# A decoder layer's expert picks: every pick loaded as one u|v double row, with a Gelu and a coefficient of its own

## What is computed

```python
def peer_ffn(xn, w_q, sub_keys, u_tab, v_tab):
    ...
        top_s, top_i = lax.top_k(s, K)                  # K = 16, for both halves of a head
        cand = top_s[:, :, 0, :, None] + top_s[:, :, 1, None, :]
        best_s, best_j = lax.top_k(cand.reshape(C, Hh, K * K), K)
        ...
        expert = ia * PEER_KEYS + ib
        g = jax.nn.softmax(best_s, axis=-1)
        u = u_tab[expert]
        a = jax.nn.gelu(jnp.einsum('cd,chkd->chk', xc, u).astype(jnp.float32), approximate=False)
        coeff = (g * a).astype(xc.dtype)
        return jnp.einsum('chk,chkd->cd', coeff, v_tab[expert])
```

## Time and profile before

| | |
|---|---|
| median of three runs | 3797.99 us (3793.36 to 3814.47) |
| span of the profiled execution | 3789.9 us, 8.1 below that median; its own time outside the trace is not listed |
| busy: TensorE, VectorE, ScalarE, GpSimd | 77%, 66%, 34%, 37% of the span |
| moved | 1297.10 MB, 342 GB/s over the span |
| queue of the gathers | 1073.83 MB, 72.2% of 16 engines' span |

### The profile page before, as it was taken

How to read it: one execution, slowest core, us unless ns; L and a number is a source line. 1 busy time by engine, 2 the same in 40 slices (tenths; PEclk the granted TensorE clock), 3 DMA queues, 4 the chain that set the end, 5 groups by cost and what they waited for, 6 DMA issues and landing times.

```text
span 3789.9 us, 34958 instructions
## 1 busy us (share of the span) xinstructions
PE 2933.6 (77%) x8920; PEld 1517.5 (40%) x8920; DVE 2484.4 (66%) x5699; ACT 1298.0 (34%) x3333; POOL 1420.4 (37%) x1367
## 2 busy tenths in 40 slices
PE   8797866984886598989689797787878777766665
PEld 6655533431443355555344343333333333322222
DVE  0321218786876477767437888877887887788765
ACT  1212312221121244444234544444443454344333
POOL 0000003443776376657423333333333333333332
PEclk9897888997898799999899999999989999999999
DMA  7844156777998999999889999999999999999998
GB/s 298 274 147 184 57 215 214 238 263 283 346 338 327 352 369 341 363 352 355 333 318 369 401 411 417 409 414 415 411 407 421 413 405 407 421 410 414 417 411 351
DMA packets 274454, 1297.10 MB, mean 342 GB/s; under 512 B 27888, under 2 KB 63088, under 8 KB 180464
## 3 DMA queue, kind: packets, MB, share of 16 engines
q0 software_dynamic: 195120, 1073.83, 72.2%
q1 hardware_dynamic: 74384, 203.74, 14.4%
q10 hardware_dynamic: 4752, 17.30, 1.2%
HBM read 1231.07 MB, written 63.70 MB: 342 GB/s over the span
## 4 chain that ended last, share of the span: by engine, by line
DMA 31%; issue 7%; DVE 5%; PE 4%; ACT 3%; POOL 0%; POOLq 0%; DVEq 0%; SPq 0%; ACTq 0%
DMA s_ring<-peer_uv,s_expert 17%; DMA e_more_slots<-peer_uv,s_expert 10%; PE e_acc L503 3%; DVE e_part L427 1%; PE e_product L1859 1%; DMA e_more_slots<-peer_v,s_expert 1%; DMA next_h<-e_h 1%; DMA e_h<-norm_ffn_row 1%; DMA s_scratch<-norm_final_row 1%; DVE s_ring L394 1%; ACT L341 1%; ACT s_diagonal L324 0%; ACT s_gate L343 0%; DVE s_dots L394 0%; DVE e_more_slots L394 0%
## 5 line engine op out<-in xcount | busy, mean ns | idle before, releaser
L503 PE MATMUL e_acc<-s_ring,s_diagonal 128*128 128x512 f32 (+1 forms) x2168 | 898.8, 543 | 379.6 <-ACT s_diagonal L324 352.8
L394 DVE CUSTOM_DVE_ANT_0 s_ring<-s_ring,e_x_copy 128x1024 f32<-128x1024 f32 x548 | 666.6, 1217 | 221.9 <-DMA s_ring<-peer_uv,s_expert 215.1
L503 PEld LDWEIGHTS e_acc<-s_ring,s_diagonal 128*128 128x128 f32 x2168 | 396.5, 199 | 943.5 <-ACT s_diagonal L324 587.5
L278 POOL DMA_INDIRECT s_ring<-peer_uv,s_expert x462 | 437.5, 947 | 783.1 <-DVE e_part L427 551.8
L278 POOL DMA_INDIRECT s_ring<-peer_u,s_expert x331 | 377.4, 1140 | 449.9 <-DVE s_expert L1796 230.8
L503 PE MATMUL e_acc<-e_more_slots,s_diagonal 128*128 128x512 f32 (+1 forms) x948 | 387.4, 536 | 153.9 <-ACT s_diagonal L324 146.3
L278 POOL DMA_INDIRECT s_ring<-peer_v,s_expert x325 | 373.2, 1148 | 332.0 <-PE e_acc L503 94.9
L341 ACT ACTIVATE s_dots<-s_dots 128x1 f32<-128x1 f32 x704 | 142.2, 202 | 961.3 <-DVE s_dots L394 959.0
L324 ACT ACTIVATE s_diagonal<-s_ident,s_gate 128x128 f32<-128x128 f32 x949 | 371.2, 399 | 223.0 <-PE e_acc L503 100.1
L278 POOL DMA_INDIRECT e_more_slots<-peer_uv,s_expert x231 | 217.6, 942 | 413.8 <-DVE e_part L427 273.5
L394 DVE CUSTOM_DVE_ANT_0 s_ring<-s_ring,s_x 128x1024 f32<-128x1024 f32 x245 | 299.5, 1222 | 104.6 <-DMA s_ring<-peer_u,s_expert 69.2
(11 more groups left out here) (233 smaller groups left out, 3618.5 us busy)
## 6 DMA issues: line engine op xcount, KB each, us to landing
w_in_kept<-w_in SPq DMA_DIRECT2D x8, 1104.0 KB, 11.8
w_in_gained<-w_in_kept SPq DMA_DIRECT2D x8, 1104.0 KB, 10.2
p_w_in<-w_in_gained SPq DMA_DIRECT2D x8, 1104.0 KB, 19.0
f_w_big<-w_mem_kv SPq DMA_DIRECT2D x4, 2048.0 KB, 19.2
f_w_big<-peer_w_q_t SPq DMA_DIRECT2D x2, 4096.0 KB, 17.9
peer_scores<-f_stage_s SPq DMA_DIRECT2D x16, 512.0 KB, 8.5
e_mem_scores<-mem_scores SPq DMA_DIRECT2D x2, 4096.0 KB, 14.6
e_mem_values<-mem_values SPq DMA_DIRECT2D x2, 4096.0 KB, 25.0
```

The source lines that it names most:

```text
L278: pool.indirect_dma_start(out=to, out_offset=None, in_=table, in_offset=bass.IndirectOffsetOnAxis(ap=self.expert[c % PICK_BUFFERS][:, k:k ...
L394: dve.tensor_tensor_reduce(row, row, x[:, :], 1.0, 0.0, ALU.mult, ALU.add, self.dots[:, k:k + 1]).then_inc(self.u_used, 1)
L503: last = pe.matmul(self.acc[:, at:to], self.diagonal[:, made % DIAGONALS, :], row[:, at:to], start=(n == group[0]), stop=(n == group[-1]))
```

## The change

- All 1024 picks come as pairs: ROWS is u0, v0, u1, v1, ...; there is no lead any more, and the tables peer_u and peer_v are gone.
- The ring holds pairs. Stages have extra slots of their own: 2 in the selection, 6 in the projection, 0 in the attention, 4 in the last. There is one semaphore for each pair of slots.
- Every pick has its Gelu and its coefficient by coeff_alone; GELU_AT and COEFF_AT are gone.
- In projection and attention VectorE adds V directly behind the product of the same pick (add_to_h). In the last stage it adds one pick later, as before.
- ScalarE gets two more places in the projection, 3 and 6. One bound of the first choices goes from 45 to 46.

```diff
-LEAD = 22
-PAIRS_FROM = 331
-ALONE_FROM = PAIRS_FROM // TOPK * TOPK
-ROWS = [("u", g) for g in range(LEAD)]
-for _g in range(PAIRS_FROM - LEAD):
-    ROWS += [("u", LEAD + _g), ("v", _g)]
...
+ROWS = [(kind, g) for g in range(TOTAL_PICKS) for kind in "uv"]
...
-            table = self.io["peer_uv" if paired else "peer_u" if kind == "u" else "peer_v"]
...
+            to = self.ring[:, slot:slot + 2, :] if slot < RING else self.more_slots[:, slot - RING:slot - RING + 2, :]
+            pool.indirect_dma_start(out=to.rearrange("p s d -> p (s d)"), out_offset=None, in_=self.io["peer_uv"],
                                     in_offset=bass.IndirectOffsetOnAxis(ap=self.expert[c % PICK_BUFFERS][:, k:k + 1], axis=0)
-                                    ).then_inc(self.row_loaded[self.slot[n]], 16)
+                                    ).then_inc(self.row_loaded[slot], 16)
...
-            if n in GELU_AT:
-                i = GELU_AT[n]
-                h = i % PEER_HEADS
-                at = slice(TOPK * h, TOPK * (h + 1))
-                act.wait_ge(self.u_used, TOPK * (i + 1))
-                act.activation(self.active[:, at], self.dots[:, at], ACT.Gelu).then_inc(self.activated, 1)
...
-            if kind == "v" and self.pe_columns(n) > 0:
-                if g >= ALONE_FROM:
-                    self.coeff_alone(g)
-                elif g % TOPK == 0 or n - 2 < self.stages[self.stage_of[n]][0]:
-                    act.wait_ge(self.coeff_ready, g // TOPK + 1)
...
+            if kind == "v":
+                self.coeff_alone(g)
+                if self.pe_columns(n) > 0:
+                    made = self.pe_through[n]
+                    need(act, self.v_pe, made - DIAGONALS)
...
-            elif self.mode(n) == "split":
-                self.wait_row(dve, n)
-                dve.wait_ge(self.coeff_ready, g // TOPK + 1)
...
+                first, end, mode = self.stages[self.stage_of[n]]
+                add = self.add_to_h if mode == "split" else self.add_part
+                if mode == "split":
+                    add(n)
+                    continue
...
+    def add_to_h(self, n):
+
+        dve = self.nc.vector
+        g = ROWS[n][1]
+        rest = slice(self.pe_columns(n), D)
+        self.wait_row(dve, n)
+        dve.wait_ge(self.coeff_made, g + 1)
+        self.wait_h(g // PICKS, self.dve_through[n] - 1)
+        dve.scalar_tensor_tensor(self.h[:, rest], self.row(n)[:, rest], self.coeff(g), self.h[:, rest], ALU.mult,
+                                 ALU.add).then_inc(self.v_dve, 1)
...
                 if more:
                     square_x(t + 1)
+                if woven:
+                    beside(stream.scalar, t, 3)
+                if more:
                     keep_x_t(t + 1)
...
+                if woven:
+                    beside(stream.scalar, t, 6)
                 act.wait_ge(q_turned, t + 1)
...
-STAGES = [(PICK_FIRST, "pe", D), (PROJECT_REST, "split", 0), (ATTEND_REST, "split", BANK), (len(ROWS), "pe", 3 * D // 4)]
+STAGES = [(PICK_FIRST, "pe", D, 2), (PROJECT_REST, "split", 0, 6), (ATTEND_REST, "split", BANK, 0), (len(ROWS), "pe", 3 * D // 4, 4)]
```

More of the change, by code:

```diff
@@ L127, in __init__ @@
         self.nc, self.io = nc, io
-        self.stages = [(start, until, mode) for start, (until, mode, _) in zip([0] + [u for u, _, _ in stages], stages)]
-        self.columns = [columns for _, _, columns in stages]
-        assert all(mode == "split" or columns == D or s == len(stages) - 1 for s, (_, mode, columns) in enumerate(stages))
+        self.stages = [(start, until, mode) for start, (until, mode, _, _) in zip([0] + [stage[0] for stage in stages], stages)]
+        self.columns = [columns for _, _, columns, _ in stages]
+        self.extra = [extra for _, _, _, extra in stages]
+        assert all(mode == "split" or columns == D or s == len(stages) - 1 for s, (_, mode, columns, _) in enumerate(stages))
         self.ident = sb("s_ident", [P, P])
@@ L171, in __init__ @@
         pe = dve = 0
-        free = list(range(RING))
+        free = list(range(0, RING, 2))
         last_in = {}
-        wide_from = self.stages[-1][0] + RING
         for n in range(len(ROWS)):
             s = next(i for i, (start, until, _) in enumerate(self.stages) if start <= n < until)
+            start, until, _ = self.stages[s]
             kind = ROWS[n][0]
@@ L231, in wait_row @@
     def wait_row(self, eng, n):
-        first = n - 1 if n >= PAIRS_AT and ROWS[n][0] == "v" else n
-        eng.wait_ge(self.row_loaded[self.slot[first]], 16 * self.loads[first])
+        eng.wait_ge(self.row_loaded[self.slot[n] // 2 * 2], 16 * self.loads[n])
     def group(self, c, s):
@@ L1549, in pick_buffers, with pick_chunks @@
     return b
-def pick_chunks(nc, io, stream, chunks, events, until, last):
+def pick_chunks(nc, io, stream, chunks, events, until, stage, last):
     with ExitStack() as ctx:
         sb, ps, sem = allocators(nc, ctx, f"_{chunks[0]}")
-        if last:
-            stream.more_slots = sb("e_more_slots", [P, WIDE_RING - RING, D])
+        if stream.extra[stage]:
+            stream.more_slots = sb("e_more_slots", [P, stream.extra[stage], D])
         mem_scores = sb("e_mem_scores", [P, DT, D])
```

113 lines of the change are left out of this document (42 added, 71 removed).

## The result

The changed kernel takes 4144.24 us (4 runs, 4138.07 to 4148.4) against 3799.88 us before: a ratio of 1.088, with an interval of 1.085 to 1.092. The forecast was 4030 us, in a range from 3880 to 4120. The side was right, the size was not: 344 us were lost where 232 were forecast, and the time lies above the range.

The account below looks back on a forecast made before the run. VectorE bounds selection, row transfers the last stage; projection and attention run close to the transfers' limit. Selection -10, projection +55, attention +187, last 0 make +232; 3789.9 + 232 + 8 = 4030 us, range 3880 to 4120.

Parts of the forecast that it names:

- The ring's pieces: Attention unit as closed loop: Exp, turning, copy, table load, Gelu, table load; 5.6 to 6.9 us, 2.5 per further V row.
- its two prices: Attention: two table loads of 1.28 us per unit, and a 2.5 us turn over VectorE per further V row.
- Rival (a): Projection and attention: row supply decides, pairs make the 490 rows 57 us faster, time 3740; chance 0.07.
- Rival (b): Attention: the 170 stalls fall into VectorE's idle time, only the projection pays, about 3850; chance 0.12.
- Rival (c): Attention: a stop as long as the load follows each of 136 further table loads, 174 us more, 4200; chance 0.03.
- ScalarE now follows VectorE pick by pick and gets 19 more table loads ... they hide: Selection: the loads, 24 us, hide because ScalarE is busy only 70 of 356 us; the stage changes by -10.
- the gain of the eleven products: Selection: VectorE does 75 products instead of 86, at 1.22 us each, 13 us less on the bounding engine.
- the projection, +55: Projection: a chunk takes 66.5 us against 55.6 because additions wait for their own coefficients; five chunks, between 0 and +90.
- the attention's sum: Attention: eighty units 500, further V rows 205, ends 38 and 25, between chunks 12, restarts 16; 796 against 609, +187.
- TensorE does not stand in the way: Attention: TensorE's 6.5 us at 1024 columns are less than the 9.4 of a unit with two V rows.
- four pairs in flight are enough: Attention: one pair is wanted every 4 to 5 us and takes 2.6 us of transfer and 1.25 on GpSimd.
- the middle parts: Whole kernel: the inner portions of the terms' bounds, giving 3910 to 4120; the range's start was lowered to 3880.

Follow-up runs that it names:

- e_copy: The changed kernel with a plain copy in place of the Gelu of picks 0 to 319, so they exchange no table; ratio 1.038.
- e_lag: The changed kernel with VectorE's addition of V in projection and attention one pick later; ratio 1.051.
- e_pelag: The changed kernel with TensorE's V multiplications of picks 0 to 74 (selection) one pick later in its order; ratio 1.087.
- e_beach: The kernel before, keeping single rows and its lead of 22 products, with a Gelu and coefficient per pick and ScalarE's two new projection places; ratio 1.045.
- e_copylag: The changed kernel with a plain copy for the Gelu of picks 0 to 319 and VectorE's addition one pick later in projection and attention; ratio 1.028.
- e_turn: The changed kernel with VectorE's picks ahead of the copy to a_mixed_t in the unit of the turning; ratio 1.088.
- e_ring3: The changed kernel with three pairs of row slots in the attention in place of four; ratio 1.098.
- e_copylag3: The changed kernel with copy for Gelu (picks 0 to 319), addition one pick later, and three pairs of row slots in the attention, not four; ratio 1.068.

## Why the prediction was right and wrong

**Right: what would bound each stage, and how.** The last stage stayed (-6, forecast between -20 and +20). In the attention VectorE's addition waits for ScalarE, the DMA share falls (0.69, forecast 0.75), 168 table loads stand on ScalarE (forecast 165). The ring's pieces are as worked out: 5.74 us at 512 columns with one pick (5.6), 9.58 at 1024 with two (9.4), a further pick 2.55 (2.5). e_copy and e_lag take its two prices away one at a time. Rival (a) fell: no gain while the ring is longer than the unit was. Rival (b) fell with the ring. Rival (c) fell by the 1.41 us that a load is worth in e_copy: what the Trainium skill ("ScalarE: Activation LUTs", What ACT_TABLE_LOAD costs) calls a drain of 1380 ns is not in these units, where 0.13 us stand beside the load.

**Wrong: the step "ScalarE now follows VectorE pick by pick and gets 19 more table loads ... they hide" as the whole account of the selection.** The step priced the late coefficient on ScalarE and not what stands behind the V row on TensorE: forecast -10, measured +21.5. e_pelag gives back 21.0 of the 31.5 between them; the other 10 are the gain of the eleven products, which shows in no run, and where it went stays open beyond the 15 us of longer waits named there. The prediction had put just this question for VectorE in the projection. "They hide" itself holds in part: e_copy takes 27 loads out of the changed kernel and gets 3.7 us, but in e_beach, where every product is ready, 15 more loads (34 for 19) and a Gelu per pick cost 13.

**Mis-sized: the projection, +55 where +75 was measured.** One p_mla_k copy to the next is 67.0, 65.7, 77.6 and 62.6 us, mean 68.2, forecast 66.5; the long one has the chunk's end in it. Before, the four have a mean of 56.4, so these chunks lost 47 us, near the 44 that the sum has for four. The rest stands at the stage's start: to the first such copy it is 100.1 us, 71.6 before, thus 28.5 more where the sum has 11 for a chunk. Ten of them are VectorE's wait for p_sin, ahead of its first product:
```profile
DVE s_ring L365 <- DMA p_sin<-sin: 28.3, 1, 28.3
```
It was 18.7 before; why it lands later wasn't tested. Taking back the late addition and the table loads gives 72 us (312 against 309 before), so the two causes named were the right ones in the main. The wait for p_sin stays 26 us in e_copylag, but the 19 us for which VectorE waited for rows in this stage before are gone.

**Mis-sized: the attention's sum, 796 where 869 (609 + 260) were measured.** 73 us are missing. The step that failed first is "TensorE does not stand in the way", with each turning put at 0.85 to 1 us; the sum also had nothing for the copy to a_mixed_t ahead of a product, and too little for the bursts. From the first Exp to the last are 79 units and 816 us. Set against the sum (5.6 to 6.9 us by width, 2.5 for each further pick) they are, with the ends:
First, the 71 units without burst or turning of a_mixed: 615 us, where the sum had 561, its 12 us between the chunks included: 54 more. 8 of them are a wait at the stage's start, for which the sum had its own term. Some 41 stand between the Exp and the copy of the turned probabilities, that is in TensorE's turning. Its group in the attention took 68.9 us before and takes
```profile
L1471 PE MATMUL a_turned<-s_ident,a_probs 128*128 128x128 f32 x480 | 96.2, 355 | 63.5 <-ACT a_probs L1271 56.0 <-ACT a_mixed_t L1286 6.9 <-DVE a_residual L1352 0.5
```
27 us more, 22 of them in these units. In one unit it is 1.09 us, in the next 1.97. The granted clock is 1.00 in the first one's window, that is 2.4 GHz throughout, and 0.60 in the second's, that is mostly the lower level of 1.2 GHz; ahead of both TensorE had idled 1.43 us for the Exp:
```profile
2149.85 1.09 PE L1471 MATMUL a_turned<-s_ident,a_probs 128*128 128x128 f32 x8 [1.43 <-ACT a_probs L1271]
...
2159.44 1.97 PE L1471 MATMUL a_turned<-s_ident,a_probs 128*128 128x128 f32 x8 [1.43 <-ACT a_probs L1271]
```
```profile
2147.00:2156.00 9.00, 6.97 (x32) 3.91 (x32) 4.84 (x8) 6.11 (x10) 2.37 (x2) 1.00 0.66 234
2157.00:2166.00 9.00, 7.57 (x19) 3.87 (x19) 4.13 (x7) 5.57 (x8) 1.96 (x2) 0.60 0.65 233
```
In a dozen units the turning also starts 0.8 to 2.1 us late, 19 us in sum, because TensorE is still at the work of the unit before, its V rows last. Here the Exp ended at 1766.7; the two multiplications take 2.02 us, in other units 1.12:
```profile
1766.76 2.02 PE L478 MATMUL a_acc<-s_ring,s_diagonal 128*128 128x512 f32 x2
1768.57 1.36 PE L1471 MATMUL a_turned<-s_ident,a_probs 128*128 128x128 f32 x6
```
Second, the four units of the turning of a_mixed: the product stands behind VectorE's copy, the coefficient behind the product, the next Exp behind the coefficient. They take 54 us, where the sum had 33 for such units: 21 more. e_turn takes 18 us out of them.
Third, the bursts: 146 us, where the sum had 129 (16 of restarts included), so 17. VectorE waits 12 us for rows in them, and the third, 49 us where the others take 29 to 36, has a chunk's end in it. So "four pairs in flight are enough" fell short here; e_ring3 and e_copylag3 show what the fourth pair is worth.
Fourth, the ends: 4 of the 869 us lie before the first Exp and 48 behind the last, where the sum had 63 and one unit more (9): 20 less.
These make 54 + 21 + 17 - 20 = 72. All four are read from the trace; a run takes out only most of the second (e_turn).

With the 31 us of the selection, the 20 of the projection and these 73 the forecast would have been 4154, for 4144 measured. The range failed in how it was put together, not in its terms' bounds: the attention (+260) lies in its +100 to +270, the projection (+75) in its 0 to +90, the selection (+21.5) just above its +20. But the range took only "the middle parts" of them, which supposes that the errors go both ways. They didn't: a coefficient that comes late lengthens all three stages, and nearly each thing left out of the sum added to it.

## What to carry to other kernels

When a coefficient moves from "made ahead" to "made behind its own product", price it on every in-order queue that takes it, not on the engine that makes it: TensorE's scores behind a V row, VectorE's next product behind an addition, and the next unit's Exp behind the last Gelu. One pick of lag between product and addition costs no memory worth naming and gave back 82 + 62 us here, since the waits then run beside each other (it holds a row's slots one pick longer). And read a sum of removed costs with care: the table loads (185) and the turn (82) together gave 176, because the rows were next in line.

## What the runs showed of the hardware beyond the forecast

TensorE became slower where it had more to wait for. It has the same 2260 multiplications in the attention window before and after, busy 534 us of 609 and 678 of 869; its granted clock fell from 0.93 to 0.80, with more of the time at 1.2 GHz and less at 2.4. Its turnings took 27 us more, its V multiplications 223 us where they took 182. Over the kernels the clock falls with the length of this stage: 0.90 in e_copy (706 us), 0.85 in e_lag (808), 0.80 in the changed kernel (891), 0.79 in e_ring3 (915). No run changes the clock by itself.

A table load on ScalarE costs 1.41 us on a path that it lies on: its own 1.28, and 0.13 because the activations around it no longer overlap.

A gather of 8 KB rows in place of two of 4 KB is worth 22 us over 170 pairs, 0.13 us a pair, where rows are waited for, and no more than 8 us where they aren't.
